# Spreading the side projection over the delta-rule scan: eight halves ahead and five late, in place of ten and three

## The reference, cut to what matters

```
def step(state, inp):
    qd, wi, ui, ai, kt, gl = inp
    v_new = ui - jnp.einsum('bhcd,bhde->bhce', wi, state)
    o = jnp.einsum('bhcd,bhde->bhce', qd, state) + jnp.einsum('bhcj,bhje->bhce', ai, v_new)
    state = state * jnp.exp(gl)[..., None, None] + jnp.einsum('bhcd,bhce->bhde', kt, v_new)
    return state, o
```

## Time and profile before

| | us |
|---|---|
| median of three runs | 2983.83 |
| the profiled execution, its own time | 2982.72 |
| span of its profile | 2980.8 |
| PE busy in the span | 2722.8 (91%) |
| DVE, POOL, ACT busy | 1593.7, 1375.6, 1130.2 |

### The profile page before, as it was taken

One profiled execution on the slowest core, in us unless ns is written; L12 is line 12 of the kernel. 1 busy time (PEld: TensorE's weight loads), 2 busy tenths in 40 slices (PEclk: granted clock), 3 DMA queues, 4 the chain that ended last, 5 costly groups with the idle time before them and its releaser, 6 DMA issues. The chain is left out here.

```text
span 2980.8 us, 40155 instructions
## 1 busy us (share of the span) xinstructions
PE 2722.8 (91%) x15402; PEld 2219.3 (74%) x15402; DVE 1593.7 (53%) x1859; ACT 1130.2 (38%) x1866; POOL 1375.6 (46%) x1226
## 2 busy tenths in 40 slices
PE   6989998999889899899879999899998899998995
PEld 4868786777768788777667787777776777896784
DVE  5137646776467443375241565377754864234743
ACT  3024434666345314331111344266653543244111
POOL 4355335343478740265354543444434886304551
PEclk8999999999989999999989999999999999999997
DMA  5253224221344556654242531333213554567431
GB/s 185 71 156 99 79 71 136 85 93 64 124 156 159 170 165 161 227 172 125 68 135 86 148 107 64 112 102 99 86 58 120 193 171 159 164 165 258 129 112 72
DMA packets 394918, 380.51 MB, mean 128 GB/s; under 512 B 91104, under 2 KB 333408, under 8 KB 394720
## 3 DMA queue, kind: packets, MB, share of 16 engines
q1 hardware_dynamic: 355744, 295.87, 33.1%
q10 hardware_dynamic: 38976, 82.00, 7.4%
HBM read 247.70 MB, written 130.09 MB: 127 GB/s over the span
## 5 line engine op out<-in xcount | busy, mean ns | idle before, releaser
L266 PE MATMUL pair<-h_hi,w_hi 128*128 128x512 f32 x1792 | 741.9, 414 | 117.3 <-ACT ev L281 44.8
L246 POOL TENSOR_TENSOR w_hi<-w_stage,masks 128x256 fp32r<-128x256 f32 x432 | 403.6, 965 | 727.3 <-PE pair L266 655.8
L266 PE MATMUL pair<-h_lo,w_hi 128*128 128x512 f32 x1792 | 710.7, 397 | 0.0
L266 PE MATMUL pair<-h_hi,w_lo 128*128 128x512 f32 x1792 | 709.9, 396 | 0.0
L266 PEld LDWEIGHTS pair<-h_hi,w_hi 128*128 128x128 f32 x1792 | 344.1, 192 | 241.7 <-issue 100.8
L266 PEld LDWEIGHTS pair<-h_hi,w_lo 128*128 128x128 f32 x1792 | 343.6, 192 | 75.7
L266 PEld LDWEIGHTS pair<-h_lo,w_hi 128*128 128x128 f32 x1792 | 344.7, 192 | 70.7 <-issue 5.1
L251 POOL TENSOR_TENSOR w_lo<-w_stage,w_hi 128x256 fp32r<-128x256 f32 x432 | 354.5, 852 | 8.5
L281 ACT ACTIVATE ev<-pair 128x512 f32<-128x512 f32 x224 | 132.6, 593 | 492.0 <-PE pair L266 491.8
L217 PE MATMUL pair<-h_hi,w_hi 128*128 128x512 f32 x576 | 183.1, 399 | 41.7 <-DVE h_lo L593 23.9
L2291 POOL TENSOR_TENSOR w_hi<-w_stage,masks 128x512 fp32r<-128x512 f32 (+1 forms) x60 | 103.6, 1727 | 221.0 <-PE pair L217 191.0
(11 more groups left out here) (283 smaller groups left out, 4940.1 us busy)
## 6 DMA issues: line engine op xcount, KB each, us to landing
w_stage<-in_w_in SPq DMA_DIRECT2D x132, 512.0 KB, 4.1
proj<-ev ACTq DMA_DIRECT2D x132, 512.0 KB, 2.7
gate<-proj SPq DMA_DIRECT2D x48, 512.0 KB, 3.6
prep_x<-proj SPq DMA_DIRECT2D x24, 512.0 KB, 4.0
resid<-xT SPq DMA_DIRECT2D x16, 512.0 KB, 8.1
diff_vx<-proj SPq DMA_DIRECT2D x16, 512.0 KB, 3.2
prep_g<-gc_rows SPq DMA_DIRECT2D x16, 512.0 KB, 5.2
qd_t<-prep_eg SPq DMA_DIRECT2D x16, 512.0 KB, 2.6
```

The lines of the kernel that those rows point to most:

```text
L246: last = nc.gpsimd.tensor_tensor(w_hi[s][:, part], w_stage[s][:, part], bcast(ones, PIECE), ALU.mult)
L266: last = nc.tensor.matmul(bank(self.banks[half]), a[s][:, c, :], b[:, c, w], start=(c == 0 and n == 0), stop=(c == KC - 1 and n == 2))
```

## The change

Four edits in `delta_rule`. Two of the ten early halves of side work move into the scan: EARLY is 8, and LATE is now 2, 3, 4, 5 and 6 in place of 1, 3 and 5, so that halves 8 to 10 stand between the stages of chunk 0 and halves 11 to 15 in those five iterations. In iteration c, SP now issues `half_inputs` for chunk c+1, as the first thing, in place of those for chunk c+2 behind the level inputs. ACT runs both copies to VW before `moves(c+1, 1)`, where the moves stood between the two.

```diff
-                EARLY, LATE, FIRST_WEIGHTS = 10, (1, 3, 5), 6
+                EARLY, LATE, FIRST_WEIGHTS = 8, (2, 3, 4, 5, 6), 6
@@ block.sync
                     for c in range(NT):
                         for d in range(2):
+                            if 1 < c + 1 < NT:
+                                half_inputs(c + 1, d)
+                        for d in range(2):
                             if c + 2 < NT:
                                 level_blocks(c + 2, d)
                                 level_inputs(sp, c + 2, d)
-                        for d in range(2):
-                            if c + 2 < NT:
-                                half_inputs(c + 2, d)
                         for d in range(2):
                             if c + 2 < NT:
                                 step_inputs(c + 2, d)
@@ block.scalar
                             nc.scalar.activation(VW[d][:], heads(E[d]), ACT.Copy).then_inc(q[f"vw{d}"], 1)
-                            if more and d == 0:
-                                moves(c + 1, 1)
                         if more:
+                            moves(c + 1, 1)
                             if c in LATE:
                                 side_out(EARLY + 3 + LATE.index(c))
                             moves(c + 1, 2)
```

## The result

| | before | changed | 
|---|---|---|
| median | 2985.16 us (4 runs, 2982.72 to 2986.74) | 3015.04 us (4 runs, 3005.31 to 3018.93) |
| profiled execution, own time | 2982.72 | 3019.76 |
| span | 2980.8 | 3017.9 |

The ratio is 1.0096 (95% interval 1.007 to 1.0121): 1.0% slower. Forecast were 3010 us, 3003 to 3016. The profiled execution of the changed kernel is 4.7 us over its median.

The account below looks back on a forecast made before the run. PE was taken to bound the scan. Late halves 22.0, earlier chunk 0 -1.0, clock 3.4, ACT 1.8 and SP 0.6 sum to +26.8 us, so 3010 us (+0.9%); range 3003 to 3016.

Parts of the forecast that it names:

- A late half costs its full length: In the scan: two more halves in each of two layers, nothing hides them, 4 x 5.50 = +22.0 us.
- The early halves were free: Ahead of chunk 0: inputs come no earlier, so removing two halves saves only the present lateness, -1.0 us.
- The clock behind the hole: After PE's idle stretch ahead of chunk 0: low clock once in each layer, +3.4 us, bounds 0 and 3.6.
- ACT's order: Iterations 0 and 1: stage-1 moves wait for the second VW copy, +2.3 us; net +1.8, bounds 0 and 4.8.
- SP's order: Iterations 1 and 2: later-issued T1 and next inputs land just in time, +0.6 us, bounds 0 and 4.
- it has landed by 1137.5: Iteration 1: T1 of chunk 2, issued 1133.9 to 1135.9, lands before `blocks(2, 2)` wants it at about 1138.1.
- the feed binds: Rival, iterations 0 and 1: T1 and chunk 3's inputs each 2.3 us late, 4.6 us a layer; 3019 us; 9%.
- Free halves: Rival, in the scan: the two extra halves fill hidden PE waits; 2985 us, no difference; 3%.
- the faster side: Rival, ahead of chunk 0: it starts when PE is free, 10.9 us gained each layer, late halves free; 2961 us; 2%.

Follow-up runs that it names:

- The counts alone: Kernel before with only EARLY = 8 and LATE = (2, 3, 4, 5, 6), SP and ACT as before: 3009.71 us, ratio 1.008.
- the filled hole: Changed kernel with 40 more matmuls of 128x512 on PE ahead of chunk 0, results thrown away: 3010.65 us, ratio 1.0077.
- the kernel with ACT's order alone: Kernel before with only both copies to VW put ahead of the moves of stage 1: 2986.0 us, ratio 1.0003.
- its repeat: Changed kernel run once more, nothing edited, beside another kernel on the same chip: 3016.73 us, ratio 1.0101.
- the kernel with both: Changed kernel with SP's order put back to that of before, run twice: 3011.86 us (ratio 1.0079) and 3012.43 us (ratio 1.0082).

## Why the prediction was right, and where a term was off

- **A late half costs its full length.** Right. Wherever PE does not wait in them, iterations with a half are 18.1 us and those without one 12.7 (13.0 with ACT's order). The counts alone give +24.5 us in the phases against 22.0 - 1.0 + 3.4 = 24.4 forecast, 21.7 of them from R of chunk 1 to R of chunk 7.
- **The early halves were free.** Right. Chunk 0 starts 55.6 and 55.8 us after the phase's first matmul, where it was 56.2 and 56.3: 1.1 us earlier in all (1.0 forecast), and holes of 9.7 and 10.2 us open.
- **The clock behind the hole.** Right in kind, and in size on average: 0.50 granted, and 1.9 us a layer by the filled hole (1.7 forecast), with 0.9 to 3.0 in single layers. The rule of the Trainium skill ("TensorE: Matmul & The Clock Gate", section "What's actually happening"), that activity releases the throttle, agrees with the window at 1.00 when the hole is filled.
- **ACT's order.** The mechanism was right, the size too large: 4 x 0.30 = 1.2 us, where 2.3 were forecast. The 0.5 us that it was to give back did come, in the kernel with ACT's order alone.
- **SP's order.** This is the mis-sized term: +0.6 us forecast (bounds 0 to 4), 9 to 11 us measured in the phases, and the sign named for it, over 1 us of idle time ahead of L2008 in iteration 1, came. The step that failed was "it has landed by 1137.5": it took the landing time of U, not of a small DMA behind 1 MB of AT and QD. The same kind of DMA, T1 in the kernel before, took up to 4.2 us. It then priced the wait alone, while the clock behind it cost 2.9 us more in layer 1 and 1.0 in layer 2. So the rival "the feed binds" had part of the loss, by T1 and not by chunk 3's inputs; no wait for those shows in the changed profile or in its repeat, which has one of 0.6 us ahead of `blocks(2, 0)`.
- **Free halves, and the faster side,** fell with the first two points.

The parts add up: the counts alone and ACT's order give 24.5 + 1.2 = 25.7 us in the phases, and the kernel with both has 25.2 and 25.1; SP's order is what the changed kernel has beyond it. The median rose by 29.9 us where 26.8 were forecast. That the total fell into the range is in part luck. In the phases the change costs 34.1 and 35.9 us, above the forecast's high end of 33.4, and 3015.04 lies a little nearer the 3019 of the rival "the feed binds" than 3010. The medians showed only 3 to 4 us of SP's 9 to 11, and why is open.

## What to carry to other kernels

Filler work is free only where the bound engine waits; so compare an iteration with it and one without before moving it, and check what ends the wait it now covers. A load moved later must be priced by its place behind the bytes ahead of it in the queues, and not by the landing time that it had before. On PE, price a wait of about 2 us or more with the low clock that may follow (1.81 us was the shortest seen with it here), and look for DMAs whose place in a program is tied to a count that is being changed.

## What the runs showed of the hardware

A wait of PE of 2.2 us was followed by a granted clock of 0.52 to 0.60 over the next 8 us, though PE was busy without a gap. Waits of much the same length do not always do this: 1.90 us without and 1.81 us with it, in one execution. The same code outside the phase took 2590.7 to 2602.6 us in the profiles of different kernels, so a difference of 5 us between two single runs does not by itself speak for or against an edit.
